# Expert loop of the last layer: the next unit's input products ahead of the unit's own outputs

## The reference

```python
def moe_ffn(h, rw, rb, w1, w3, w2, sw1, sw3, sw2):
    ...
    # top 8 of 64 experts for each token; gate: (tokens, 64), zero where not chosen
    a = jnp.einsum('td,edh->teh', h, w1)        # w1, w3: (64, 1024, 128)
    b = jnp.einsum('td,edh->teh', h, w3)
    act = (jax.nn.silu(a) * b * gate[..., None].astype(h.dtype))
    routed = jnp.einsum('teh,ehd->td', act, w2)  # w2: (64, 128, 1024)
    shared = (jax.nn.silu(h @ sw1) * (h @ sw3)) @ sw2
    return (routed + shared).astype(h.dtype)
```

## Time and profile before

| | us |
|---|---|
| median of 3 runs | 1337.35 |
| lowest and highest run | 1326.41, 1337.71 |
| the profiled execution's own time | 1331.15 |
| its span, first to last instruction | 1329.3 |
| TensorE busy in the span | 1179.0 (89%) |
| VectorE busy | 600.6 (45%) |
| ScalarE busy | 272.6 (21%) |
| GpSimd busy | 279.1 (21%) |
| DMA: queue of the weights, share of 16 engines | 62.2% |
| mean granted clock of TensorE, as a share of full speed | 0.957 |

### The profile page before, as it was taken

How to read it: one execution, slowest core, us unless ns; L and a number is a source line. 1 busy time by engine, 2 the same in 40 slices (tenths; PEclk the granted TensorE clock), 3 DMA queues, 4 the chain that set the end, 5 groups by cost and what they waited for, 6 DMA issues and landing times. The chain is left out here.

```text
span 1329.3 us, 20780 instructions
## 1 busy us (share of the span) xinstructions
PE 1179.0 (89%) x7406; PEld 614.6 (46%) x7406; DVE 600.6 (45%) x1395; ACT 272.6 (21%) x665; POOL 279.1 (21%) x358
## 2 busy tenths in 40 slices
PE   4899999898999899998789889999987799898883
PEld 1443445344464455654345454485544444444331
DVE  5311725267568422222223218575367654344445
ACT  0100013234312122221112101313512111121110
POOL 1000102334403233332223300103612211110000
PEclk9899999999999899998889899999997899899987
DMA  9965604855284699999999979443147999999970
GB/s 331 377 249 201 214 1 138 274 196 208 82 319 175 243 397 410 410 389 382 402 393 396 377 285 381 144 173 80 48 146 285 347 379 407 408 407 404 402 297 34
DMA packets 112846, 372.01 MB, mean 280 GB/s; under 512 B 16026, under 2 KB 22460, under 8 KB 106584
## 3 DMA queue, kind: packets, MB, share of 16 engines
q1 hardware_dynamic: 90728, 311.92, 62.2%
q0 software_dynamic: 20416, 55.39, 11.2%
q10 hardware_dynamic: 1584, 3.21, 0.6%
HBM read 361.99 MB, written 26.30 MB: 292 GB/s over the span
## 5 line engine op out<-in xcount | busy, mean ns | idle before, releaser
L1500 PE MATMUL bank<-weights,b_qk 128*32 128x256 f32 (+2 forms) x1280 | 127.3, 385 | 4.7 <-DMA weights<-in_exp_w 2.1
L2502 DVE TENSOR_TENSOR expert_act<-silu_a,bank 128x128 f32<-128x128 f32 x42 | 12.1, 288 | 209.4 <-ACT silu_a L1849 209.4
L1500 PEld LDWEIGHTS bank<-weights,b_qk 128*32 128x32 f32 (+2 forms) x1280 | 76.5, 125 | 54.0 <-issue 28.6
L1521 PE MATMUL bank<-weights,expert_act_T 128*32 128x512 f32 (+2 forms) x320 | 77.3, 656 | 21.8 <-DMA weights<-in_exp_w 17.8
L2788 POOL DMA_INDIRECT shift_scale_gate_norm<-scratch_h,gather_index x72 | 75.0, 1042 | 63.9 <-POOL gather_index L2785 59.8
L1290 PE MATMUL bank<-weights,features_h 128*128 128x512 f32 x192 | 84.3, 594 | 2.3 <-DMA weights<-in_w_out 1.5
L2741 POOL TENSOR_SCALAR mod_rows_and_probs<-mod_rows_and_probs,prob_recip 128x512 f32<-128x512 f32 (+1 forms) x36 | 48.4, 1353 | 147.8 <-DVE prob_recip L2231 147.7
L1489 PE MATMUL bank<-tab,shift_scale_gate_norm 128*128 128x128 f32 x544 | 72.4, 277 | 7.2 <-DMA shift_scale_gate_norm<-scratch_h,gather_index 7.2
L1849 ACT ACTIVATE silu_a<-bank 128x128 f32<-128x128 f32 x66 | 18.3, 277 | 277.8 <-PE bank L1500 277.8
L2492 DVE COPY b_qk<-bank 128x512 f32<-128x512 f32 x68 | 47.0, 692 | 54.4 <-PE bank L1489 54.4
L1489 PEld LDWEIGHTS bank<-tab,shift_scale_gate_norm 128*128 128x128 f32 x544 | 66.4, 191 | 10.4 <-issue 8.5
(11 more groups left out here) (379 smaller groups left out, 2141.8 us busy)
## 6 DMA issues: line engine op xcount, KB each, us to landing
weights<-in_exp_w SPq DMA_DIRECT2D x171, 512.0 KB, 13.6
features_h<-in_exp_w SPq DMA_DIRECT2D x52, 512.0 KB, 12.5
qkv<-in_exp_w SPq DMA_DIRECT2D x52, 512.0 KB, 15.6
shift_scale_gate_norm<-in_ada_w SPq DMA_DIRECT2D x24, 1024.0 KB, 8.2
c_padded<-in_exp_w SPq DMA_DIRECT2D x39, 512.0 KB, 14.4
a_q<-in_exp_w SPq DMA_DIRECT2D x26, 512.0 KB, 12.7
weights<-in_w_in SPq DMA_DIRECT2D x6, 2048.0 KB
filters<-in_exp_w SPq DMA_DIRECT2D x19, 512.0 KB, 15.6
```

The source lines that it names most:

```text
L1500: mm = pe.matmul(ab[r, 0:2 * HIDDEN].rearrange("p (m h) -> p m h", m=2), XGT[:, u.slot() % 2, k, r], expert_w13(slot)[:, :, k, :], start=k ...
L1521: mm = pe.matmul(yp[h][r, :], ACTT[:, r], expert_w2(slot)[:, h * HALF:(h + 1) * HALF], start=True, stop=True)
```

## The change

Nothing but TensorE's program order changes, and only in the last layer (`summed`). Before, unit n on TensorE goes: products(n), combine(n-1, 0), act_T(n), tokens_T(n+1), second(n, 0), combine(n-1, 1), second(n, 1). After the change products(0) comes first, and then unit n goes: combine(n-1, 0), act_T(n), tokens_T(n+1), products(n+1), second(n, 0), combine(n-1, 1), second(n, 1). The orders of ScalarE, VectorE, POOL and SP stay as they are, and so do all waits.

```diff
-                for n, (_, listed) in enumerate(SEQUENCE[l]):
+                places = [[(x % ring_n, x // ring_n + 1, r) for x, _, r in listed] for _, listed in SEQUENCE[l]]
+                for n, experts in enumerate(places):
                     u = At(0, n)
-                    was, experts = (experts if n else None), [(x % ring_n, x // ring_n + 1, r) for x, _, r in listed]
-                    products(u, experts)
+                    if n == 0 or not summed:
+                        products(u, experts)
                     if n and summed:
                         combine(At(0, n - 1), 0)
                     elif n:
-                        second(At(0, n - 1), was, 1, first=n == 1)
+                        second(At(0, n - 1), places[n - 1], 1, first=n == 1)
                     act_T(u)
                     tokens_T(At(0, n + 1))
+                    if summed and n + 1 < every:
+                        products(At(0, n + 1), places[n + 1])
                     second(u, experts, 0, first=n == 0)
                     if n and summed:
                         combine(At(0, n - 1), 1)
```

## The result

The changed kernel takes 1360.27 us (median of 3 runs, 1357.96 to 1363.67). Its ratio to the kernel before is 1.0219, 95% interval 1.0176 to 1.0262: slower. Whether it is slower by more than 2% the interval leaves open. The two medians alone would give 1.017; the three runs of the kernel before lie 11.3 us apart, so I go by the ratio. The forecast was 1360, with a range of 1345 to 1378. The profiled execution took 1363.67 us with a span of 1361.8.

The account below looks back on a forecast made before the run. TensorE's work early and the expert-weight stream later were taken as close limits; 49.5 us of new waits less 28.2 in hand gave +21.3, plus 7 for the clock on 1331.15 and 1 for the median: 1360 us, range 1345 to 1378.

Parts of the forecast that it names:

- What was in hand: Last layer's expert loop: 18.8 us of weight waits plus some 9.4 us of slower-clock matmuls, 28.2 us to set against new waits.
- The activation's wait: TensorE ahead of the transposed activation: VectorE still runs the activation behind both subtractions, a new 1.3 us in every unit.
- The tokens' wait: TensorE ahead of the next products: they must wait for VectorE's copy of the transposed tokens, 0.84 us in every unit.
- The weight queue: SP's queue: w13 slots return earlier, w2 slots later, one partly holding the other; cost nothing, ten-slot ring as cover.
- The clock: TensorE in the expert loop: new waits drop it to the lower clock in some units, 4.4 x 1.6 = +7 us.
- my one in five: Assumed share of units whose waits bring the lower clock, 4.4 units at 1.6 us; bounds were never and all 22.
- the stretch at 1286: Trace from 1286 to 1293 us: 1.1 us of transposes and 1.20 us without work, clock 1.00; read as against per-unit falls.
- The sum: Whole expert loop: 49.5 us of new waits less 28.2 in hand, +21.3 us, plus 7 for the clock.
- the stream stays the bound and the change gains: Rival for the expert loop: new waits under 1.2 us a unit vanish in weight waits, about 1327 or 1328; 6 in 100.
- The gain of 3.6 us at the end: End of the loop: the last unit's products run during the last w2 wait, so their 3.6 us block drops out.
- only one wait is real: Rival for the two new TensorE waits: tokens' copies hidden, 30 us against 28.2, no change, 1331 to 1338; 7 in 100.
- the clock falls in every unit: Rival for TensorE in the expert loop: lower clock each unit, +35 us, 1387 up to 1394 us; 9 in 100.

Follow-up runs that it names:

- Experiment 1: Changed kernel with VectorE taking the next unit's activation between its split of half 0 and its copy of half 1; ratio 1.0029 to the kernel before.
- experiment 2: Changed kernel with the next unit's products one step later on TensorE, behind the outputs of half 0; ratio 1.0014 to the kernel before.
- experiment 7: Changed kernel reordered: token transposes first, products ahead of both outputs, ScalarE and VectorE orders adapted, transposed activation in the output bank; ratio 0.9995 to the kernel before.
- experiment 9: Changed kernel with early activation, products behind the outputs of half 0, and last-layer w2 four experts behind w13 instead of two; ratio 1.0016 to the kernel before.
- experiment 6: Kernel before with two extra matmuls, 0.86 us a unit, ahead of the transposed activation; ratio 0.9998.
- experiment 8: Tokens-first kernel (token transposes first, products ahead of outputs) with last-layer w2 four experts behind w13 instead of two; ratio 0.9989 to the kernel before.

## Why the prediction was right

**What was in hand, 28.2 us.** Confirmed by itself: 23 x 2.15 us of added work made the loop 20.7 us longer (49.5 - 28.2 = 21.3 by the prediction), and 23 x 0.86 us made the time no longer by more than the noise of 3 us. The runs' ratio alone would allow 26 to 40 us.

**The activation's wait, 1.3 us.** It measured 1.22 us a unit, put down to VectorE's activation. Experiment 1 moved nothing but that activation and took the wait away. The prediction had the activation start at 2.2 us after the last output, and it was 2.1; the subtraction and the activation overlap a little (1088.03 and 1088.64, 0.61 us apart, where I had counted the full 0.69).

**The tokens' wait, 0.84 us.** It measured 0.96 us, and experiment 2 took it away alone. VectorE's copy ended where the prediction had it, 1.79 us after the start of the transposes (1090.30 + 0.69 = 1090.99), but the products followed it by 0.16 us, not by the 0.05 that I had read from another pair of instructions. Together 2.18 against the 2.15 of the sum; with the slower start of the transposes a cycle is 11.73 us instead of the 11.6 of the prediction.

**The weight queue, nothing.** Right for the time: no wait for weights appeared. But I had said that w2 slots would only partly hold the queue up. In fact SP waits 65.1 us for them and 39.2 for the products. It cost nothing here, as TensorE is later still. That the ring of ten slots is the cover fits this, but no run with fewer slots shows it.

**The clock, +7 us.** It measured 4 stretches and 6.8 us (products of 5.36 us instead of 3.67, so 1.69 each), where the prediction took 4.4 at 1.6. That the sizes agree is in part luck. The same kernel had eight such stretches in another execution, and the three loops with the same cycle of 11.72 to 11.74 us read 282.1, 289.1 and 295.4 us with none, four and eight of them: (289.1 - 282.1) / 4 = 1.75 and (295.4 - 282.1) / 8 = 1.66 us each. So the price of one is well known; how many there are is not, and my one in five had no better basis than lying between two rows. That filling one of the two waits removes them is shown in one profiled execution, and by the mean clock of all four of its runs. The ratio fell by 0.006 (8 us) with it; the intervals of the two ratios overlap.

Two readings around this term held less than I made of them. In the kernel before, each wait for weights of 2.35 us and more was followed by the lower clock, but in other kernels single waits of 2.35 (experiment 7), 2.56 (experiment 9), 2.83 (experiment 1) and 3.39 us (experiment 6) were not. And the stretch at 1286 hardly spoke against the rule on transposes: by that rule it had 2.25 us without work (1.05 + 1.20), less than the shortest wait that was followed by the lower clock.

**The sum.** 21.3 + 7 = 28.3 us was forecast for the loop, 30.7 came. The rest is 22 x 0.1 us from the cycle. From there to 1360 I added 1 us for a median that stood 6.2 us above the profiled execution. The changed kernel's median is 3.4 us below its profiled execution instead, so that the total agrees within 0.3 us is luck; the 28.3 against 30.7 us of the loop is the fair measure. The low end of the range was also mis-stated: waits a quarter shorter would be 49.5 x 0.75 - 28.2 = 8.9 us, or 1340, and not the 1346 that I gave.

**The rivals.** That the stream stays the bound and the change gains needed less than 1.2 us more a unit. Experiments 1 and 2 had cycles of 10.43 and 10.77 us, 0.95 and 1.29 us more than the 9.48 before, and showed what comes at this edge: no loss to speak of, and no gain. The gain of 3.6 us at the end, which that rival promised, didn't come in any kernel. Its reason was half right. The last products do come ahead of the outputs that had waited for the last w2, but the outputs of the unit before then stand behind the last wait for w13, and in the profiled execution of experiment 8 the two cancelled. That only one wait is real was refuted by the two experiments; that the clock falls in every unit, by the four and eight stretches in 23 units.

**What stays open.** Why the stretches come in some units and not in others of the same cycle. And whether tokens first with the later w2 gains anything: the interval of its ratio, 0.9964 to 1.0013, includes the 3.6 us, though its one profiled loop is only 0.3 us shorter.

## What to carry to other kernels

When a block of work moves forward on one engine, ask who was working under its cover, and in what order: here a VectorE instruction whose input came 3.7 us earlier still ran at the same place of its own program. A software pipeline is one order per engine, and all of them have to move together; with both covers restored the same idea cost nothing, and gained nothing either. And before paying for a gain on one engine, measure what it has in hand against the other limit: dummy work added to the kernel before (0.86 us a unit free, 2.15 us a unit 20.7 us dearer) gives that in two runs, and would have said here that there was no gain to be had while the weights' stream set the end.

## What the runs showed of the hardware that I had not expected

Waits of 1.06 and 0.89 us, with 1.06 us of transposes between, are enough to bring TensorE's clock from 2.4 to 1.2 GHz for 3.4 us in some units (four of 23 in one execution, eight in another), while a single wait of 1.20 us behind such transposes didn't. Filled with 0.8 us of matmuls whose results nobody reads, the same cycle kept 1.00 in all 275 us. The length of a wait alone doesn't decide it: a single one of 2.35 us was followed by the lower clock in the kernel before, and one of 3.39 us in experiment 6 was not:

```profile
1290.58 0.59 PE L1521 MATMUL bank<-c_padded,expert_act_T 128*32 128x512 f32 x1 [3.39 <-DMA weights<-in_exp_w]
1285.00:1300.00 15.00, 11.44 (x80) 6.44 (x80) 4.76 (x8) 1.75 (x4) 0.00 (x0) 1.00 0.18 71
```

The Trainium skill says, in TensorE: Matmul & The Clock Gate, section Part 4: PE-mode transpose, that transposes don't count as busy in the way matmuls do. These runs neither show nor refute it. By that rule a unit of the changed kernel has 3.01 us without work (1.06 + 1.06 + 0.89), and the lower clock followed in four and eight of 23 units. But the wait of 3.39 us came right behind 1.04 us of transposes, which makes 4.4 us by that rule, and the lower clock did not follow it.

Added work first ate the waits for weights and, with them, the time at the lower clock that followed them (six stretches down to one, then none). Of the 28 us in hand 9 were of this second kind. So a wait for weights can cost more than its own length.
